# Block 2's attention: one VectorE step placed behind the maxima of the first two heads

## The chip, the cores and the metric

The kernel runs on one core of a Trainium2 chip. The time is device time in microseconds of one execution; lower is better. The kernel before takes 1686.93 us, the median of three runs (1686.88 to 1688.33).

## What is computed

Two blocks of a sequence model in float32, 256 tokens of width 1024. The second block has two layers with a context stream of another 256 tokens; only layer 0 updates the context. The part that matters is each layer's attention with eight heads: queries and keys of 96 features, the last 32 of which are turned by a rotary embedding, then softmax and a weighted sum.

```python
def apply_axial_rope(u, cos, sin):
    def rot(p):
        h = p.shape[-1] // 2
        return jnp.concatenate([-p[..., h:], p[..., :h]], axis=-1)
    rotated = jnp.concatenate([rot(u[..., :AXIS_DIM]), rot(u[..., AXIS_DIM:])], axis=-1)
    return (u.astype(jnp.float32) * cos + rotated.astype(jnp.float32) * sin).astype(u.dtype)
...
    def attend(qblk):
        logits = jnp.einsum('bqhd,bkhd->bhqk', qblk, k).astype(jnp.float32) * SM_SCALE
        p = jax.nn.softmax(logits, axis=-1).astype(v.dtype)
        return jnp.einsum('bhqk,bkhd->bqhd', p, v)
```

In layer 0 the latent queries see 512 keys and the context queries 256; in layer 1 there are latent queries alone. Next to the attention each layer has two convolution branches whose taps run on VectorE.

## The kernel before

Each engine has its own instruction stream, written out by hand, and the streams meet at semaphores ("flags"). All weights come as 460 pieces of 512 KB through a ring of eight slots, loaded by SyncE. For block 2 the streams are `l2_pe` (TensorE), `l2_act` (ScalarE) and `l2_dve` (VectorE), called once for each layer, `l` = 0 and 1. The functions named below are local to them.

**TensorE.** The up-projections write queries, keys and values; `rotations(g)` (L1749) multiplies four heads' queries (g = 0: heads 0 to 3, g = 1: heads 4 to 7) by a constant matrix into PSUM banks 4, 5 or 6, 7. Then comes a loop over heads `i` (16 in layer 0, 8 in layer 1): `scores(i + 2)`, `turned(i)`, every second time `out_pair(i - 2)`, and steps of the convolution branches (`branch_pe`). `scores(i)` (L1815) writes the scores of a head for two blocks of 128 queries into banks 0, 1 (even heads) or 2, 3 (odd heads); from head 2 on it waits for the exponentials of head i - 2 (`p_exp`), and before head 4 for the second rotation (`q_rotated`). `turned(i)` (L1825) transposes the probabilities into banks 4 and on; it waits for `p_ready` of head i. `out_pair` (L1838) multiplies by the values into bank 6, and the branch step `mean` (L1847) writes bank 7; both wait for `rotation_read`, the flag that VectorE has read the second rotation. `mean` stands behind `turned(1)` in layer 0 and behind `turned(0)` in layer 1.

**ScalarE.** `exp(i)` (L1986) takes the exponentials of a head from PSUM with the negative maximum as bias; it waits for `s_max` of head i. The loop copies the transposed probabilities to SBUF (L2032) and then does `exp(i + 2)`.

**VectorE.** `top(i)` waits for the scores (`s_ps`), takes the maxima of both query blocks in one reduction (L2206) and scales them (L2207, `s_max`). `normalised(i)` waits for `p_exp`, takes a reciprocal (L2212) and scales the probabilities (L2214 twice, `p_ready`). `rotate(g, step)` applies the rotation of four heads in three pieces of 32 partitions by 1024 elements: piece 0 (L2266) multiplies the TensorE product in PSUM by the sines into a scratch tile and waits until it is done, piece 1 (L2269) multiplies the queries by the cosines, piece 2 (L2271) adds the two. Convolution taps are L2098, L2104 and L2105; L337 splits a piece of weights. The order is that of the code:

```python
        rotate(1, 0)
        top(0)
        top(1)
        normalised(0)
        rotate(1, 1)
        for i in range(len(L.heads)):
            if i + 2 < len(L.heads):
                top(i + 2)
            if i + 1 < len(L.heads):
                normalised(i + 1)
            if i == 0:
                rotate(1, 2)
```

In front of this stand the first rotation (`rotate(0, 0)` to `rotate(0, 2)`) and the last taps. VectorE runs its instructions in this order, so an instruction that waits holds everything behind it.

Of the kernel before, what the change touches and what calls it, by code (L numbers as in the profile page):

```python
# [149 lines left out]
def program(nc, xT_in, ctxT_in, weights, params_in, shared_in, hyb_in, out):  # L150
# [144 lines left out]
    def flag(name):  # L295

        if name not in flags:
            flags[name] = sem(name)
        return flags[name]
# [1777 lines left out]
    def l2_dve(dve, link, L):  # L2077
# [31 lines left out]
        def do_taps(n):  # L2109
            for _ in range(min(n, len(taps))):  # L2110
                f, i, j = taps.pop(0)

                other = next((q for q, t in enumerate(taps) if t[:2] != (f, i)), 0)
                if taps:
                    taps.insert(0, taps.pop(other))
                if (f, i) in tap_of:
                    dve.wait_ge(flag("taps"), tap_of[f, i])
                tap_done.append(0)
                tap_of[f, i] = len(tap_done)
                f(i, j).then_inc(flag("taps"), 1)  # L2120
# [81 lines left out]
        def top(i):  # L2202
            n = 4 if L.heads[i][0] == 0 else 2
            dve.wait_ge(flag("s_ps"), L.at + i + 1)
            two = slice(2 * i, 2 * i + 2)
            link(nc.vector.tensor_reduce(c_soft[:, 0, two], psum[:, 2 * (i % 2):2 * (i % 2) + 2, 0:n * P], AX.X, ALU.max))  # L2206
            nc.vector.tensor_scalar(c_soft[:, 1, two], c_soft[:, 0, two], -SM_SCALE, None, ALU.mult).then_inc(flag("s_max"), 1)  # L2207

        def normalised(i):
            n = 4 if L.heads[i][0] == 0 else 2  # L2210
            dve.wait_ge(flag("p_exp"), 2 * (L.at + i + 1))
            link(nc.vector.reciprocal(c_soft[:, 3, 2 * i:2 * i + 2], c_soft[:, 2, 2 * i:2 * i + 2]))  # L2212
            for b in range(2):
                last = nc.vector.tensor_scalar(c_p[:, i % 2, b, 0:n * P], c_p[:, i % 2, b, 0:n * P],  # L2214
                                               c_soft[:, 3, 2 * i + b:2 * i + b + 1], None, ALU.mult)
            last.then_inc(flag("p_ready"), 1)
# [41 lines left out]
        def rotate(g, step):  # L2258

            q = c_Q[R, 4 * g:4 * g + 4, 0:SEQ]  # L2260
            turned = psum[R, 4 + 2 * g:6 + 2 * g, :].rearrange("p b c -> p (b c)").rearrange("p (h t) -> p h t", h=4)
            t = normed[R, :, :].rearrange("p a b -> p (a b)").rearrange("p (h t) -> p h t", h=4)
            four = lambda ap: ap.unsqueeze(1).broadcast_to([QK - NOPE, 4, SEQ])
            if step == 0:
                dve.wait_ge(flag("q_rot"), 2 * l + g + 1)
                nc.vector.tensor_tensor(t, turned, four(sin2), ALU.mult).then_inc(flag("rotation_read"), 1)  # L2266
                dve.wait_ge(flag("rotation_read"), 2 * l + g + 1)
            if step == 1:
                link(nc.vector.tensor_tensor(q, q, four(cos2), ALU.mult))  # L2269
            if step == 2:  # L2270
                link(nc.vector.tensor_tensor(q, q, t, ALU.add))  # L2271
                dve.sem_inc(flag("q_rotated"), 1)

        for i in range(3):
# [3 lines left out]
                    rotate(0, step)  # L2278
                branch_dve("taps")
            do_taps(6)  # L2280
        rotate(1, 0)
        top(0)
        top(1)
        normalised(0)
        rotate(1, 1)
        for i in range(len(L.heads)):
# [57 lines left out]
    with nc.Block() as block:  # L2344
# [91 lines left out]
        @block.vector  # L2436
        def _(dve):
            link = Link(dve, dve_step)
            hyb_dve(dve, link)
            layer_norm_dve(dve, link, 0, 0, "ln1_g", "ln1_b", 0, None)  # L2440
            lo_split(dve, U_MLP1 + WIDE_FIRST)
            link(nc.vector.tensor_scalar(y[:, :, 0:SEQ], x[:, :, 0:SEQ], ALPHA, None, ALU.mult))
            mlp_dve(dve, link, 0, U_MLP1, SEQ)
            layer_norm_dve(dve, link, 1, 1, "ln2_g", "ln2_b", 1, None)
            lo_split(dve, U_REC + WIDE_FIRST)
            rec_dve(dve, link, 1)
            layer_norm_dve(dve, link, 2, 2, "ln1_g", "ln1_b", 3, None)
            lo_split(dve, U_MLP2 + WIDE_FIRST)
            link(nc.vector.tensor_scalar(y[:, :, 0:SEQ], x[:, :, 0:SEQ], ALPHA, None, ALU.mult))
            mlp_dve(dve, link, 1, U_MLP2, SEQ)  # L2450
            layer_norm_dve(dve, link, 3, 3, "ln2_g", "ln2_b", None, U_L2 + LEAD)
            for L in LAYERS:
                modulated_dve(dve, L.norm, SEQ, L.split)
                l2_dve(dve, link, L)
                gated_dve(dve, link, L.norm + 1, L.T)
                modulated_dve(dve, L.norm + 2, L.T, L.split + 2)
                lo_split(dve, U_L2MLP[L.l] + WIDE_FIRST)
                dve.wait_ge(x_ready, KT * (L.split + 4))
                link(nc.vector.memset(y[:, :, 0:L.T], 0.0))
                mlp_dve(dve, link, 2 + L.l, L.base + L2_IN + 3 + KT, L.T)  # L2460
                gated_dve(dve, link, L.norm + 3, SEQ)
                if L.l == 0:
                    late_added_dve(dve)
# [198 lines left out]
```

## Time and profile before

| | |
|---|---|
| median of three runs | 1686.93 us |
| the runs | 1686.88 to 1688.33 us |
| the profiled execution's own time | 1687.68 us |
| its span (first to last instruction) | 1685.8 us |
| mean granted TensorE clock | 0.986 |
| TensorE busy | 1606.9 us (95%) |
| VectorE busy | 1027.2 us (61%) |
| ScalarE busy | 838.2 us (50%) |

The profile is of one execution. A row of the timeline gives start, duration, engine, line, operation, output and inputs, and in brackets the idle time before it with what ended it. The chain of waits is the work that ended last, followed back from the last instruction: each piece is what released the next one. PE is TensorE, DVE is VectorE, ACT is ScalarE. The granted clock is a share of TensorE's full clock of 2.4 GHz.

### The profile page before, as it was taken

The numbers are of one execution on the slowest core, as the hardware profiler recorded it, in microseconds if no ns is written. First come the engines' busy times: TensorE is split into PE (matmuls) and PEld (weight loads), VectorE is DVE, ScalarE is ACT, GpSimd is POOL, SyncE is SP. The second block draws the span as 40 slices with busy tenths as digits, with TensorE's granted clock in tenths as the row PEclk, the third lists the DMA queues.
The fourth block names the chain that finished last, engine by engine and source line by source line (L and its number), as shares of the span: only waits on it lengthen the run. The fifth ranks groups of instructions, "written<-read, shape, count | busy, mean of one in ns | idle before, by whom it ended". The sixth has DMA issues, their size and how long they took to land.

```text
span 1685.8 us, 25551 instructions
## 1 busy us (share of the span) xinstructions
PE 1606.9 (95%) x10226; PEld 1379.5 (82%) x10226; DVE 1027.2 (61%) x1616; ACT 838.2 (50%) x1484; POOL 76.6 (5%) x60
## 2 busy tenths in 40 slices
PE   7998999999999999999889999999999989889997
PEld 7887789998889999988557588888888875779996
DVE  6855765567676566769864643333333688565665
ACT  5434275554726566453684551514243555665554
POOL 1200300001031000000000100000000100100000
PEclk9999999999999999999999999999999999999999
DMA  8733665556746555543101532222222241235551
GB/s 302 264 115 138 251 235 176 187 187 225 264 174 221 180 188 187 180 158 100 63 1 63 212 101 97 91 100 87 100 100 88 67 146 38 68 122 178 185 186 50
DMA packets 69937, 247.49 MB, mean 147 GB/s; under 512 B 7504, under 2 KB 10576, under 8 KB 69712
## 3 DMA queue, kind: packets, MB, share of 16 engines
q1 hardware_dynamic: 69840, 246.18, 42.7%
q8 instruction: 63, 1.03, 0.3%
q14 instruction: 34, 0.28, 0.1%
HBM read 245.10 MB, written 1.05 MB: 146 GB/s over the span
## 4 chain that ended last, share of the span: by engine, by line
PE 75%; DVE 12%; issue 7%; ACT 4%; DMA 0%; POOL 0%; DVEq 0%; SPq 0%; ACTq 0%; POOLq 0%
PE psum L376 15%; PE psum L378 15%; PE psum L377 15%; PE psum L397 9%; PE psum L398 5%; DVE lo_ring L337 3%; PE psum L1143 2%; PE psum L1815 2%; PE psum L411 1%; DVE c_conf L2098 1%; PE psum L412 1%; PE psum L413 1%; PE psum L1825 1%; PE psum L1838 1%; PE psum L511 1%
## 5 line engine op out<-in xcount | busy, mean ns | idle before, releaser
L376 PE MATMUL psum<-x_parts,hi_ring 128*128 128x256 f32 (+1 forms) x1464 | 460.9, 315 | 12.3 <-DVE x_parts L902 9.9
L337 DVE TENSOR_TENSOR lo_ring<-raw_ring,hi_ring 128x1024 fp32r<-128x1024 f32 x348 | 432.6, 1244 | 60.2 <-PE psum L378 21.1
L377 PE MATMUL psum<-x_parts,hi_ring 128*128 128x256 f32 (+1 forms) x1464 | 456.1, 312 | 0.0
L378 PE MATMUL psum<-x_parts,lo_ring 128*128 128x256 f32 (+1 forms) x1464 | 455.9, 311 | 0.0
L349 ACT ACTIVATE hi_ring<-raw_ring 128x1024 fp32r<-128x1024 f32 x292 | 307.3, 1053 | 256.7 <-PE psum L378 137.7
L376 PEld LDWEIGHTS psum<-x_parts,hi_ring 128*128 128x128 f32 x1464 | 281.2, 192 | 34.2 <-issue 16.4
L377 PEld LDWEIGHTS psum<-x_parts,hi_ring 128*128 128x128 f32 x1464 | 281.4, 192 | 14.9 <-issue 0.2
L378 PEld LDWEIGHTS psum<-x_parts,lo_ring 128*128 128x128 f32 x1464 | 281.2, 192 | 14.8
L397 PE MATMUL psum<-hid_parts,hi_ring 128*128 128x512 f32 x672 | 235.2, 394 | 0.3 <-DVE lo_ring L337 0.3
L1420 DVE TENSOR_TENSOR hid_parts<-relu,hid_parts 128x256 fp32r<-128x256 f32 (+1 forms) x128 | 63.1, 493 | 221.1 <-ACT relu L1409 221.1
L398 PE MATMUL psum<-hid_parts,lo_ring 128*128 128x256 f32 x672 | 188.3, 280 | 0.0
L397 PEld LDWEIGHTS psum<-hid_parts,hi_ring 128*128 128x128 f32 x672 | 126.5, 188 | 29.2 <-DVE lo_ring L337 0.6
L2390 POOL TENSOR_SCALAR hi_ring<-raw_ring 128x1024 fp32r<-128x1024 f32 x56 | 76.4, 1366 | 1403.0 <-DMA raw_ring<-weights 637.7
L1406 ACT ACTIVATE relu<-psum 128x256 f32<-128x256 f32 (+1 forms) x128 | 55.7, 435 | 162.5 <-PE psum L378 149.4
L398 PEld LDWEIGHTS psum<-hid_parts,lo_ring 128*128 128x128 f32 x672 | 125.9, 187 | 0.0
L376 PE MATMUL psum<-hid_parts,hi_ring 128*128 128x512 f32 (+1 forms) x320 | 115.1, 360 | 0.0
L378 PE MATMUL psum<-hid_parts,lo_ring 128*128 128x512 f32 (+1 forms) x320 | 114.6, 358 | 0.0
L377 PE MATMUL psum<-hid_parts,hi_ring 128*128 128x512 f32 (+1 forms) x320 | 113.7, 355 | 0.0
L1449 DVE TENSOR_TENSOR y<-psum,y 128x512 f32<-128x512 f32 (+1 forms) x44 | 26.2, 595 | 110.1 <-PE psum L378 96.6
L411 PE MATMUL psum<-x_parts,hi_ring 128*128 128x256 f32 (+1 forms) x184 | 59.7, 324 | 14.8 <-DVE x_parts L1195 9.0
L1443 DVE TENSOR_TENSOR y<-psum,y 128x256 f32<-128x256 f32 x84 | 35.7, 425 | 59.1 <-PE psum L398 53.8
L2098 DVE SCALAR_TENSOR_TENSOR c_conf<-c_u,par,c_conf 128x512 f32<-128x512 f32 (+1 forms) x120 | 68.3, 617 | 0.9
(430 smaller groups left out, 2338.2 us busy)
## 6 DMA issues: line engine op xcount, KB each, us to landing
raw_ring<-weights SPq DMA_DIRECT2D x460, 512.0 KB, 3.4
h_const<-hyb_consts SPq DMA_DIRECT2D x1, 1088.0 KB, 11.4
x<-xT SPq DMA_DIRECT2D x1, 1024.0 KB, 6.9
x<-ctxT SPq DMA_DIRECT2D x1, 1024.0 KB, 16.6
outT<-x SPq DMA_DIRECT2D x4, 256.0 KB, 2.5
shared<-shared_consts SPq DMA_DIRECT2D x1, 398.0 KB, 13.3
par<-params SPq DMA_DIRECT2D x1, 301.5 KB, 7.0
```

The source lines that it names most:

```text
L337: nc.vector.tensor_tensor(lo_ring[:, s, :], raw_ring[:, UNIT_AT[u] % RAW_SLOTS, :], hi_ring[:, s, :].bitcast(F32), ALU.subtract).then_inc( ...
L349: nc.scalar.activation(hi_ring[:, SPLIT[v] % SPLIT_SLOTS, :], raw_ring[:, slot, :], ACT.Copy).then_inc(act_hi_ready, 1)
L376: nc.tensor.matmul(bank(u % BANKS, T), w_hi, hi[:, hi_place[k], 0:T], start=(k == 0), stop=False)
L377: nc.tensor.matmul(bank(u % BANKS, T), w_hi, lo[:, k, 0:T], start=False, stop=False)
L378: last = nc.tensor.matmul(bank(u % BANKS, T), w_lo, hi[:, hi_place[k], 0:T], start=False, stop=(k == KT - 1))
L397: nc.tensor.matmul(side_by_side(u), w_hi, parts[:, :, k, 0:SEQ], start=(k == 0), stop=False)
L398: last = nc.tensor.matmul(bank(u % BANKS, SEQ), w_lo, parts[:, 0, k, 0:SEQ], start=False, stop=(k == KT - 1))
L411: nc.tensor.matmul(bank(v % BANKS, T), w_hi, hi[:, hi_place[k], 0:T], start=(k == order[0]), stop=False)
L1406: nc.scalar.activation(relu[:, j % 2, 0:T], bank(u % BANKS, T), ACT.Relu).then_inc(drained[u % BANKS], 1)
L1420: nc.vector.tensor_tensor(hid_lo[:, j, 0:T], relu2[:, j % 2, 0:T], hid_hi[:, j, 0:T].bitcast(F32), ALU.subtract).then_inc(flag("hidden_rea ...
L2098: return nc.vector.scalar_tensor_tensor(acc, src, w, acc, ALU.mult, ALU.add)
L2390: nc.gpsimd.tensor_scalar(hi_ring[:, n % SPLIT_SLOTS, :], raw_ring[:, slot, :], 1.0, 0.0, ALU.mult, ALU.add).then_inc(hi_ready, 1)
```

## The change

In `l2_dve`, for both layers, piece 0 of the second rotation moves behind the maxima of heads 0 and 1.

```diff
             do_taps(6)
-        rotate(1, 0)
         top(0)
         top(1)
+        rotate(1, 0)
         normalised(0)
         rotate(1, 1)
```

## Rows read from the trace of the kernel before

**Rows 1.** The page: busy time by engine (part 1), the chain by engine (part 4).
```profile
PE 1606.9 (95%) x10226; PEld 1379.5 (82%) x10226; DVE 1027.2 (61%) x1616; ACT 838.2 (50%) x1484; POOL 76.6 (5%) x60
...
PE 75%; DVE 12%; issue 7%; ACT 4%; DMA 0%; POOL 0%; DVEq 0%; SPq 0%; ACTq 0%; POOLq 0%
```

**Rows 2.** Chain of waits, layer 1: start us, us, engine, tile, line.
```profile
1410.15 1.23 DVE normed L2266
...
1411.41 1.24 DVE c_soft L2206
...
1412.87 1.46 ACT c_p L1986 x4
...
1414.37 3.78 PE psum L1815 x4
...
1425.76 1.06 PE psum L1825 x8
...
1434.99 1.02 ACT c_pT_low L2032
```

**Rows 3.** Chain of waits, layer 0.
```profile
831.57 1.24 DVE c_soft L2206
...
833.10 0.88 DVE c_p L2214 x2
...
834.01 1.23 DVE c_Q L2269
...
835.26 1.24 DVE c_soft L2206
...
836.52 0.17 DVE c_soft L2207
...
836.79 0.89 DVE c_p L2214 x2
...
837.82 1.06 PE psum L1825 x8
...
856.88 1.02 ACT c_pT_low L2032
```

**Rows 4.** Timeline of all engines, layer 0.
```profile
828.39 1.22 DVE L2266 TENSOR_TENSOR normed<-psum,shared 32x1024 f32<-32x1024 f32 x1
...
829.93 1.23 DVE L2206 TENSOR_REDUCE c_soft<-psum 128x2 f32<-128x1024 f32 x1 [0.32 <-PE psum L1815]
...
832.89 1.98 PE L1815 MATMUL psum<-c_K,c_Q 96*128 96x512 f32 x4 [1.36 <-ACT c_p L1986]
```

**Rows 5.** Timeline of all engines, layer 1.
```profile
1408.05 3.70 PE L1815 MATMUL psum<-c_K,c_Q 96*128 96x512 f32 x8 [1.48 <-DVEq L2272]
...
1414.35 0.17 DVE L2212 RECIPROCAL c_soft<-c_soft 128x2 f32<-128x2 f32 x1 [0.18 <-ACT c_p L1986]
1414.37 3.78 PE L1815 MATMUL psum<-c_K,c_Q 96*128 96x512 f32 x4 [2.62 <-ACT c_p L1986]
```

**Rows 6.** Busy time by stretch: columns as in the first line.
```profile
core 0: us, PE busy (x) PEld busy (x) DVE busy (x) ACT busy (x) POOL busy (x), PEclk, DMA share, GB/s
831.55:832.89 1.34, 0.00 (x0) 0.00 (x0) 1.29 (x2) 1.29 (x4) 0.00 (x0) 1.00 0.00 0
832.89:840.50 7.61, 7.26 (x29) 4.02 (x30) 7.23 (x14) 4.86 (x10) 0.00 (x0) 1.00 0.00 0
862.18:864.83 2.65, 0.00 (x0) 0.00 (x0) 0.00 (x0) 2.64 (x6) 0.00 (x0) 1.00 0.00 0
864.83:868.24 3.41, 3.37 (x12) 2.91 (x13) 2.20 (x7) 3.02 (x7) 0.00 (x0) 0.50 0.00 0
...
1411.75:1414.37 2.62, 0.00 (x0) 0.00 (x1) 2.37 (x5) 1.50 (x5) 0.00 (x0) 1.00 0.00 0
1414.37:1421.20 6.83, 6.83 (x16) 4.39 (x17) 5.08 (x10) 2.59 (x6) 0.00 (x0) 0.50 0.00 0
```

## The prediction

> **What bounds the kernel now.** I read the page's busy times and its chain first, to see which engine ends the kernel; then the chain of waits and the timeline over the start of block 2's attention in each of its two layers; last the granted clock there. TensorE is busy 95% of the span and holds 75% of the chain, VectorE 61% and 12% [rows 1]. Averaged so, VectorE looks harmless. But at the start of attention there are no scores yet, TensorE has nothing else to do, and the chain passes through VectorE. The change sits there, and the two layers must be read apart, because in them the moved step meets opposite conditions.
>
> Layer 1 (around 1410 us): VectorE is late. It runs the step to be moved, rotate(1, 0), from 1410.15, then the maxima of head 0 at 1411.41; these release ScalarE's exponentials (1412.87), and these release the scores of head 2 (1414.37) [rows 2]. All of this is on the chain, and TensorE idles 2.62 us before the scores of head 2 [rows 5].
>
> Layer 0 (around 830 us): VectorE is early. It starts rotate(1, 0) at 828.39 and then still waits 0.32 us for the scores of head 0 before the maxima at 829.93 [rows 4]. So the step is hidden under TensorE's first scores. From 831.57 the chain leaves TensorE and runs through VectorE alone: maxima of head 1, normalising of head 0, rotation, maxima of head 2, normalising of head 1, up to the transposes of head 1 at 837.82 [rows 3].
>
> **The change part by part.** Nothing is added or removed: one VectorE instruction (1.22 us, 1.26 from its start to the next one's, 1410.15 to 1411.41 [rows 2, 4]) changes its place in the queue, together with its two waits. The wait for TensorE's rotation matmuls is met in both places: the step starts at 828.39 and 1410.15 with no idle time shown before it, and its new place is later. The wait for its own completion travels with it and lies inside the 1.26. The bank that it reads is released later, but the matmuls that need this bank also stand behind transposes that need normalised probabilities, and VectorE gives those only after the step. No DMA and no other queue is moved; the weight stream moves nothing in the listed stretches (0 GB/s) [rows 6].
>
> *Layer 0: a loss of 1.26.* In front, taking the step away gives nothing: the maxima of head 0 wait for the scores anyway. Behind the maxima of head 1 (which end with the small scaling after 831.57 + 1.26) the step stands in the VectorE chain and pushes each later item by 1.26: normalising of head 0 from 833.10 to 834.36, transposes of head 1 from 837.82 to 839.08 [rows 3]. Behind the step now queue the normalising of head 0, whose transposes TensorE waits for, and the maxima of head 2, which ScalarE waits for. From 837.82 the chain holds only TensorE up to 856.88, where ScalarE takes over from it [rows 3]; there is no slack that could take the 1.26 back. Bounds: nothing below zero, since nothing starts earlier, and 1.26 above. I take 1.26, because the chain has no idle time to absorb it.
>
> *Layer 1: a gain.* The maxima of head 0 move from 1411.41 to 1410.15, for the scores of head 0 are there by then: TensorE began its eight score instructions at 1408.05 and needs 3.70 for both heads [rows 5], half of it by 1409.90. The exponentials of head 0 then come at 1411.61 instead of 1412.87 and the scores of head 2 at 1413.11 instead of 1414.37: 1.26 earlier. The idle time of TensorE shrinks from 2.62 to 1.36. The maxima of head 1 wait for their scores until 1411.77 (1408.05 + 3.70), and the step follows; it ends at about 1414.45, and normalising of head 0, which stood at 1414.35 waiting for exponentials [rows 5], moves by 0.1 only. So the step now fills time in which VectorE waited.
>
> The second part of the gain depends on the clock. In the kernel before the granted clock is 1.00 during the 2.62 us of idle and 0.50 (1.2 GHz instead of 2.4) from 1414.37 to 1421.20 [rows 6]: the scores of head 2 take 3.78 there against 1.98 for the same four instructions in layer 0 [rows 4, 5]. In layer 0 TensorE idles 1.36 at this very place and the clock stays at 1.00 [rows 4, 6]. With the change layer 1 has layer 0's idle time, so I take it that the clock stays up. Then VectorE becomes the chain, item by item from layer 0's starts [rows 3]: from 1411.77 maxima of head 1 with scaling 1.45, the step 1.26, normalising 1.10, rotation 1.25, maxima of head 2 1.26, normalising with its preparation 1.16, rotation 1.25, maxima of head 3 1.26, normalising 1.16, and 0.14 to TensorE: the transposes of head 2 start at 1423.06 instead of 1425.76 [rows 2], a gain of 2.70. From there the chain of before has only TensorE until ScalarE at 1434.99 [rows 2], which moves with it. If the clock falls all the same, the gain is the 1.26 of the earlier start. Bounds: 1.26 and 2.70; I take 2.70, by the row nearest to it, the idle time of 1.36 in layer 0 at full clock.
>
> *What the skill would say.* The Trainium skill ("TensorE: Matmul & The Clock Gate", A second HAM failure mode: psum-queue depth-cycling) tells of a kernel in which frequent short idle times between groups of matmuls that cycle through PSUM banks made the clock swing; the scores here cycle through two pairs of banks. By that page the sum would be 0.0 rather than -1.4; layer 0's stretch speaks against it.
>
> *Sum.* 1.26 - 2.70 = -1.44. The profiled execution took 1687.68 (span 1685.8), 0.75 above the median of 1686.93; its own time would become 1686.24. The change of -1.44 set against the median gives **1685.5 us**.
>
> **The rivals.**
> *A: the clock falls in layer 1 anyway*, after idle times of 1.48 and 1.36 so close together [rows 5]. Then +1.26 - 1.26 = 0: 1686.9. For it: the first of the two gaps has no counterpart in layer 0. Against it: layer 0.
> *B: nothing moves, because VectorE isn't the engine that counts.* The Trainium skill ("Perfetto Trace Analysis", Identifying the Most-Contended Engine) wants the engine with the highest occupancy improved first, which by the page of the profile is not VectorE. Time: 1686.9. Against it: the chain names VectorE at both places [rows 2, 3]; only an exact cancelling gives this time, which is A.
> *C: a further half-clock stretch goes.* In layer 0 TensorE idles 2.65 from 862.18 and then has 0.50 until 868.24 [rows 6]. Work that comes 1.26 later may meet the clock otherwise. Such a stretch, 3.37 busy at half clock, is worth 1.7: 1683.8; with a second one 1682.1.
> *D, slower: the clock falls in layer 0.* The step opens new idle time of TensorE before the transposes of heads 0 and 1, about 0.7 and 1.1, behind the 1.36. If this brings 0.50 as in layer 1, a stretch of 6.83 [rows 6] costs up to 3.4; with layer 1's sure 1.26 this is +1.26 + 3.4 - 1.26: 1690.3; half of that stretch 1688.6. It decides where the clock after 832.89 is below 1.00. Against it: each gap is at most 1.36, which the row shows harmless alone.
>
> **How the numbers follow.** Forecast 0.52; A 0.22; B 0.03; C 0.14; D 0.09. The three times shown differ by up to 1.45 (1686.88 to 1688.33), so a median can be off by half that, 0.7. A measurement can tell about 0.2%, 3.4 us, from no change. The range goes from C's 1683.8 less 0.7, 1683.1, to D's milder 1688.6. Faster by over 3.4 needs C with a second stretch or with the spread: 0.09. Slower by over 3.4 needs D in full: 0.04. The rest, 0.87, is no measurable change.
>
> **What would show it.** Right: in layer 1 the maxima of head 0 start at about 1410.15 plus layer 0's shift, TensorE's idle time before the scores of head 2 is near 1.36, the clock from there on is 1.00, and the transposes of head 2 come 2.7 earlier against the first scores. In layer 0 the transposes of head 1 come at about 839.1 with some 1.1 idle before them, chained to VectorE. Wrong: a clock of 0.50 behind the scores of head 2 (A), or behind 832.89 (D); transposes of head 1 in layer 0 still at 837.8; or an equal time in which both layers moved by other amounts than these.

## The result, and the profile after

The kernel after takes 1689.02 us, the median of 20 runs (1685.88 to 1695.10); the kernel before beside it takes 1686.18, also 20 runs (1682.89 to 1689.17). The ratio is 1.0023, with a 95% interval of 1.0014 to 1.0032: slower by 2.4 to 5.4 us, 2.8 by the medians. The forecast was 1685.5, and its range ended at 1688.6: wrong in sign and outside the range.

The profiled execution took 1686.86 (span 1684.9, mean granted clock 0.986), which is 0.8 less than that of before and 2.2 less than its own median. So one trace against one trace shows the wrong sign here. What hides it lies in front of the change: the last piece of the first rotation in layer 0, up to which both kernels run the same instructions, starts at 824.34 after and at 826.13 before, and from there to the end of the span the traced execution after takes 860.6 against 859.6. The reading below therefore goes by stretches in several traces. The page of after, engines and chain (answers to [rows 1]):

```profile
PE 1605.9 (95%) x10226; PEld 1377.0 (82%) x10226; DVE 1027.1 (61%) x1616; ACT 838.1 (50%) x1484; POOL 75.2 (4%) x60
...
PE 79%; DVE 9%; issue 7%; ACT 4%; DMA 1%; POOL 0%; SPq 0%; DVEq 0%; ACTq 0%; POOLq 0%
```

VectorE's share of the chain fell from 12% to 9% and TensorE's busy time by 1.0. Both look like progress. The chain of waits after, both layers (answers to [rows 2, 3]):

```profile
829.78 1.24 DVE c_soft L2206
...
831.24 1.23 DVE normed L2266
...
832.70 0.38 DVE c_p L2214
...
1406.29 3.71 PE psum L1815 x8
...
1410.03 1.24 DVE c_soft L2206
...
1411.49 1.23 DVE normed L2266
...
1413.86 1.23 DVE c_Q L2269
```

In both layers the moved step (L2266) is now a link of the chain: in layer 0 it was not one, in layer 1 it was one before the maxima and is one behind them. The timeline after, of all engines (answers to [rows 4, 5]):

```profile
828.07 1.22 DVE L2206 TENSOR_REDUCE c_soft<-psum 128x2 f32<-128x1024 f32 x1 [1.61 <-PE psum L1815]
...
831.04 0.17 DVE L2207 TENSOR_SCALAR c_soft<-c_soft 128x2 f32<-128x2 f32 x1
...
831.24 1.22 DVE L2266 TENSOR_TENSOR normed<-psum,shared 32x1024 f32<-32x1024 f32 x1
...
837.42 1.06 PE L1825 MATMUL psum<-shared,c_p 128*128 128x128 f32 x8 [0.97 <-DVE c_p L2214]
...
1406.29 3.70 PE L1815 MATMUL psum<-c_K,c_Q 96*128 96x512 f32 x8 [1.48 <-DVEq L2272]
...
1411.36 1.98 PE L1815 MATMUL psum<-c_K,c_Q 96*128 96x512 f32 x4 [1.36 <-ACT c_p L1986]
...
1412.75 0.17 DVE L2212 RECIPROCAL c_soft<-c_soft 128x2 f32<-128x2 f32 x1
...
1416.37 0.17 DVE L2207 TENSOR_SCALAR c_soft<-c_soft 128x2 f32<-128x2 f32 x1
...
1416.45 0.16 DVE L2212 RECIPROCAL c_soft<-c_soft 128x2 f32<-128x2 f32 x1
...
1421.48 1.06 PE L1825 MATMUL psum<-shared,c_p 128*128 128x128 f32 x8 [0.61 <-DVE c_p L2214]
...
1439.05 1.39 PE L1825 MATMUL psum<-shared,c_p 128*128 128x128 f32 x8 [2.85 <-DVE c_p L2214]
...
1440.37 3.25 PE L1838 MATMUL psum<-c_pT_low,c_v 128*64 128x256 f32 x16
```

The same place in the trace of before, behind the same idle time:

```profile
1443.34 1.06 PE L1825 MATMUL psum<-shared,c_p 128*128 128x128 f32 x8 [2.85 <-DVE c_p L2214]
1444.33 1.95 PE L1838 MATMUL psum<-c_pT_low,c_v 128*64 128x256 f32 x16
```

Where the step was taken away in layer 0, VectorE now only waits (1.61 before the maxima of head 0). In layer 1 the scores of head 2 take 1.98 again behind 1.36 of idle time, as forecast. But behind the transposes of head 6 the products with the values take 3.25; in the trace of before the same 16 take 1.95. Busy time by stretch after, columns as in [rows 6]:

```profile
826.15:832.89 6.74, 5.46 (x13) 2.01 (x11) 4.67 (x8) 2.90 (x9) 0.00 (x0) 1.00 0.00 0
831.03:837.42 6.39, 4.79 (x17) 2.21 (x17) 6.11 (x12) 3.57 (x8) 0.00 (x0) 1.00 0.00 0
...
1411.36:1421.48 10.12, 8.71 (x33) 4.50 (x33) 9.64 (x18) 6.04 (x13) 0.00 (x0) 1.00 0.00 1
...
1439.65:1443.06 3.41, 3.41 (x19) 1.92 (x19) 1.76 (x5) 2.20 (x5) 0.00 (x0) 0.50 0.02 5
...
1487.44:1494.26 6.82, 5.83 (x27) 5.86 (x28) 4.18 (x9) 6.38 (x13) 0.00 (x0) 0.50 0.00 1
```

The half-clock stretch behind the scores of head 2 is gone, and two stand further on that the trace of before does not have: at the transposes of head 6 and at the beginning of layer 1's MLP.

To compare whole stretches, the starts of the same VectorE instruction (at 1501, of a wait) are taken in every trace. The times below are differences of such starts, named by their place in the trace of before. Layer 0's first stretch goes from the last piece of the first rotation (826.13) to the last piece of the second (837.70); layer 1's goes from the tap behind the first rotation (1408.08) to the maxima of head 3 (1423.20).

| stretch (us of before) | before | after |
|---|---|---|
| 826 to 837, start of layer 0's attention | 11.58 | 12.96 |
| 857 to 900, its end | 42.87 | 44.50 |
| 1408 to 1423, start of layer 1's attention | 15.12 | 12.59 |
| 1423 to 1441 | 17.70 | 17.71 |
| 1441 to 1450, transposes of head 6 | 9.93 | 11.56 |
| 1450 to 1476 | 25.20 | 25.20 |
| 1476 to 1490, second normalisation | 14.18 | 14.48 |
| 1490 to 1501, beginning of the MLP | 11.05 | 12.49 |
| 1408 to 1501 together | 93.18 | 94.03 |

So layer 1 gains 2.53 at its start and gives back 1.63, 0.30 and 1.44 before 1501, 3.37 in all.

### The profile page after: what moved, and what is told of

The parts are those of the page before. It is cut to its first block, busy times and chain, and to the rows that moved or that the text cites. A ratio compares the mean times of both kernels' runs of the same rounds, so it can differ in the third digit from the quotient of the medians.

```text
span 1684.9 us, 25551 instructions
## 1 busy us (share of the span) xinstructions
PE 1605.9 (95%) x10226; PEld 1377.0 (82%) x10226; DVE 1027.1 (61%) x1616; ACT 838.1 (50%) x1484; POOL 75.2 (4%) x60
## 4 chain that ended last, share of the span: by engine, by line
PE 79%; DVE 9%; issue 7%; ACT 4%; DMA 1%; POOL 0%; SPq 0%; DVEq 0%; ACTq 0%; POOLq 0%
PE psum L376 16%; PE psum L378 15%; PE psum L377 15%; PE psum L397 9%; PE psum L398 5%; PE psum L1143 2%; PE psum L424 2%; PE psum L411 2%; DVE lo_ring L337 2%; PE psum L413 1%; PE psum L412 1%; PE psum L1815 1%; PE psum L1838 1%; PE psum L511 1%; PE psum L1825 1%
```

## The experiments

Three theories were to be told apart. **Order:** layer 1 is faster by its new order, and what is lost is layer 0's 1.39 and work elsewhere. **Clock:** layer 1's shorter start is nothing but the missing half-clock stretch, and half-clock stretches that come later instead take it back. **Scatter:** the later stretches differ from execution to execution whatever the order. The expectations on record name their theories by letters; what a letter stands for is told by what it expects. All ratios are against the kernel before, run beside it on the same chip, with 95% intervals.

### One layer at a time, and the kernel after again

```diff
-        rotate(1, 0)
+        if l != 0:
+            rotate(1, 0)
         top(0)
         top(1)
+        if l == 0:
+            rotate(1, 0)
```

This is layer 0 alone; the kernel for layer 1 alone has 1 in place of 0. The kernel after ran beside them.

> The step moves in layer 0 alone. Theory P (the arithmetic of the prediction, and the rest is elsewhere): +1.3 us. Theory Q (in some executions the clock falls at the start of layer 0's attention, because the moved step opens new idle time of TensorE there): +3 us or more in the median, with single executions 5 us and more above the others. Theory R (the clock falls in layer 1 instead): +1.3 us.

> The step moves in layer 1 alone. Theories P and Q: faster by 1.3 to 2.7 us, and without executions far above the others. Theory R: slower by 1.5 us or more, with single executions 5 us above.

> The changed kernel once more, for another trace and other executions. All theories: about +2.8 us against before, single executions at 1692 us or more; if the trace is of one of these it shows where the half-clock stretch lies (Q: behind 830 us, R: behind 1410 us, P: in neither).

| | median us (range, runs) | ratio |
|---|---|---|
| before | 1686.25 (35 runs) | |
| layer 0 alone | 1688.62 (1683.42 to 1692.66, 12) | 1.0014 [1.0001, 1.0027] |
| layer 1 alone | 1686.49 (1682.53 to 1690.58, 12) | 1.0001 [0.9989, 1.0012] |
| after, again | 1691.22 (1683.57 to 1694.05, 12) | 1.0018 [1.0004, 1.0032] |

The part in layer 0 is slower, by an interval that just leaves out no change; the part in layer 1, forecast to gain 2.70, shows no gain. For layer 1 alone none of the three theories had forecast an equal time. The start of layer 0's attention takes 12.96 with layer 0 alone and 11.57 with layer 1 alone: the 1.39 belongs to layer 0's move. In layer 1 alone the start of layer 1's attention took 14.28 and not 12.59, because this time the clock was halved earlier, at the first scores. Its timeline:

```profile
1406.14 5.40 PE L1815 MATMUL psum<-c_K,c_Q 96*128 96x512 f32 x8 [1.48 <-DVEq L2272]
```

The eight took 5.40 instead of 3.70. The transposes of head 6 cost 1.63 more there too, and 1408 to 1501 took 94.06, against 93.19 with layer 0 alone, where layer 1 has the old order.

### Filling the idle time before the scores of head 2

```diff
         scores(1)
+        for f in range(3):
+            nc.tensor.matmul(psum[:, 4, :], c_Q[0:QK, 0, 0:P], c_K[0:QK, 0, 0:TB], start=True, stop=True)
```

Here the kernel after has three more matmuls in each layer, whose result nobody reads, so that TensorE does not idle before the scores of head 2.

> The changed kernel with three matmuls whose output nobody reads behind the scores of head 1, in both layers: they fill the idle time of 1.3 us before the scores of head 2 and add no wait. Theories Q and R: the executions at 1692 us and more go, and the median comes to 1.4 us below before or lower. Theory P: the spread stays, the median stays at +2.8 us or is a little above.

1687.84 (1683.26 to 1692.83, 12 runs), ratio 1.0011 [0.9998, 1.0025]: between before and after, and not told from either. Its trace again has half clock at the first scores (start 14.28) and at the transposes of head 6 (11.56), and 1408 to 1501 takes 95.59. Filling this one place does not keep the clock up.

### Single traces: how much differs without any change

The kernel before was traced twice more, layer 1 alone, layer 0 alone and the kernel after once more each. No edit; one time each.

> The kernel before, for a second trace. Theory S (in layer 1 the old order lets the clock fall at the scores of head 2, and then not at the second long idle time, in front of the transposes of head 6; with the step moved it falls there instead): half clock behind the scores of head 2 and 1.00 behind the transposes of head 6, as in the first trace; the first scores of layer 1 to the copy of the last head pair take 42.5 us. Theory U (where the clock falls is a matter of the single execution and has nothing to do with the order): in this trace it may fall at either place, at both or at none.

> The kernel before, for a third trace. Theory V says where half clock can be, at the idle times of 2.6 to 3.1 us, but not in which execution. If the old order ties its places together (theory S): half clock behind the scores of head 2 in layer 1 and none at the second normalisation behind the attention, as in both traces so far.

> The step moves in layer 1 alone, for a second trace. Theory S: 1.00 behind the scores of head 2, half clock behind the transposes of head 6, about 1.6 us given back there. Theory U: either.

> The step moves in layer 0 alone, second trace. Theories X and V: 1.39 us lost between the step's place and the probabilities of head 1. Behind it, from 857 to 892 us: if the new order makes more half clock there, 28.5 us or more between the maxima of head 5 and those of the last head (with 26.9 where the clock stays up); if it is a matter of the execution alone, about as often 26.9 as 28.3 or more.

> The changed kernel, third trace. Layer 0 as in the run before it. Layer 1, theory X: no half clock behind the scores of head 2, half clock at the transposes of head 6, and from the last instruction of the first rotation to the second normalisation's end 93.9 us or more (before: 93.2 to 93.4 in four traces).

The times were 1684.95 (before again), 1688.84 (before, third), 1685.82 (layer 1 alone), 1691.47 (layer 0 alone) and 1690.21 (after, third). The table puts all traces in which the idle times at head 6 and behind are not filled beside each other; head 2 filled is the kernel of the last experiment. The stretch from 826 to 837 has no column: it is 11.57 or 11.58 with the old order in layer 0 and 12.96 or 12.97 with the new one, in every trace.

| trace | 857 to 900 | 1372 to 1395 | 1408 to 1423 | 1441 to 1450 | 1490 to 1501 | 1408 to 1501 | 1372 to 1501 |
|---|---|---|---|---|---|---|---|
| before | 42.87 | 22.87 | 15.12 | 9.93 | 11.05 | 93.18 | 128.53 |
| before again | 43.11 | 21.50 | 13.81 | 11.48 | 11.05 | 93.40 | 127.39 |
| before, third | 42.88 | 22.86 | 15.11 | 9.94 | 11.06 | 93.20 | 128.54 |
| layer 0 alone | 41.63 | 22.87 | 15.13 | 9.92 | 11.05 | 93.19 | 128.54 |
| layer 0 alone, again | 47.22 | 21.52 | 15.14 | 9.93 | 11.05 | 93.23 | 127.24 |
| after | 44.50 | 21.55 | 12.59 | 11.56 | 12.49 | 94.03 | 128.07 |
| after, again | 45.63 | 21.57 | 12.59 | 11.56 | 12.47 | 93.93 | 127.98 |
| after, third | 41.64 | 21.36 | 14.28 | 11.56 | 12.47 | 95.65 | 129.49 |
| after, filled | 41.64 | 21.34 | 14.28 | 11.56 | 12.46 | 95.59 | 129.41 |
| layer 1 alone | 44.46 | 21.34 | 14.28 | 11.56 | 11.04 | 94.06 | 127.88 |
| layer 1 alone, again | 43.03 | 21.53 | 12.59 | 11.56 | 11.23 | 93.00 | 127.01 |
| head 2 filled | 44.50 | 22.87 | 12.44 | 11.56 | 12.56 | 94.10 | 129.45 |

The stretches of layer 1 are coupled. In the four traces with the long stretch behind the scores of head 2 (start 15.1) the transposes of head 6 keep full clock (9.9), and in all eight others they don't (11.5 to 11.6). From 1408 to 1501 the five traces with the old order and nothing filled take 93.2 to 93.4, the six with the new one 93.0 to 95.7, 94.4 on average. A part of that difference is not the order's: the half clock at the first scores (14.28) comes before the step's place makes any difference, and in layer 1 alone nothing in front of it is changed; it goes with a shorter stretch further up, 21.34 to 21.36 from 1372 to 1395. Counted from 1372 the means are 128.05 and 128.31, and the ranges overlap (127.24 to 128.54 and 127.01 to 129.49). So by the means the gain of 2.5 at the start is taken back in full, and by how much more lies between 0.3 and 1.1; from so few traces it may also be nothing.

Much of the scatter arises in front of the change: the last piece of the first rotation in layer 0, with only the same instructions in front of it, starts between 823.61 and 829.49 in these twelve traces. From there to the end of the span the three traces of before take 857.4 to 859.8 and the three of after 860.6 to 861.7, 2.1 more by the means.

Scatter is real, then, but it is not the whole: head 6 loses its full clock in every trace with the new order. Before again shows the exchange without any change: its half-clock stretch at head 2 is half as long, and the second one comes at head 6. Its busy time by stretch:

```profile
1411.57:1414.98 3.41, 3.41 (x6) 1.24 (x6) 2.07 (x3) 1.07 (x4) 0.00 (x0) 0.50 0.00 0
1438.88:1442.29 3.41, 3.27 (x16) 2.41 (x18) 1.37 (x4) 2.42 (x6) 0.00 (x0) 0.50 0.00 0
```

After, third, shows a clock that was halved at the first scores. Busy time by stretch:

```profile
1408.85:1412.25 3.40, 3.40 (x5) 1.35 (x4) 2.24 (x4) 0.00 (x0) 0.00 (x0) 0.50 0.02 5
...
1442.98:1446.40 3.42, 3.42 (x18) 2.05 (x17) 1.59 (x5) 2.28 (x5) 0.00 (x0) 0.50 0.00 0
1490.77:1497.60 6.83, 5.79 (x27) 5.82 (x28) 4.18 (x9) 6.36 (x13) 0.00 (x0) 0.50 0.00 1
```

The end of layer 0's attention (857 to 900) takes 42.9 to 44.5 in the six traces above with the old order there, and 41.6 to 47.2 with the new one. In layer 0 alone, again, two full stretches at half clock stand in it:

```profile
868.66:875.50 6.84, 6.62 (x16) 4.46 (x17) 3.03 (x9) 5.14 (x14) 0.00 (x0) 0.50 0.01 2
892.55:899.38 6.83, 6.05 (x24) 3.32 (x21) 2.53 (x6) 3.04 (x6) 0.00 (x0) 0.50 0.00 0
```

The spread is wider with the new order; whether its mean is higher can't be told from six traces a side.

### Filling the idle times behind

First, in the kernel with layer 1 alone, the long idle time before the transposes of head 6: a step of the convolution branch moves there, led by five matmuls whose result nobody reads.

```diff
-                 {0: ["mean"], 3: ["sums"], 4: ["sc"], 7: ["again"]}]
+                 {0: ["mean"], 3: ["sums"], 5: ["sc"], 7: ["again"]}]
...
+        def idle_fill(b, n):
+            for _ in range(n):
+                nc.tensor.matmul(psum[:, b, 0:2 * P], c_Q[0:QK, 4, 0:P], c_K[0:QK, 0, 0:2 * P], start=True, stop=True)
...
                 pe.wait_ge(flag("branch_rstd"), 2 * l + 1)
+                idle_fill(7, 5 if l else 0)
```

> The step moves in layer 1 alone, and there the sums of the short convolution's squares move from head 4 to behind the transposes of head 5, led by five matmuls that nobody reads, so that TensorE has work in the long idle time in front of the transposes of head 6. Theory S: the clock stays up there, the 1.6 us come back: 1.5 to 2.5 us faster than before, and the trace shows 1.00 from 1410 to 1450. Theory U: 1.3 us faster than before or less; equal to the variant without it.

1684.45 (1681.55 to 1690.11, 12 runs), before 1686.36, ratio 0.9994 [0.9983, 1.0005]: not told from before. In its trace (lines moved by four) the idle time before the transposes of head 6 is 0.69 and they run at full clock:

```profile
1436.43 1.06 PE L1829 MATMUL psum<-shared,c_p 128*128 128x128 f32 x8 [0.69 <-DVE c_p L2219]
1437.42 1.95 PE L1842 MATMUL psum<-c_pT_low,c_v 128*64 128x256 f32 x16
```

The 1.63 is gone: 1423 to 1450 takes 27.63, as before (17.70 + 9.93), against 29.27 after. But 1476 to 1490 now takes 15.47 instead of 14.18, with half clock from 1474.63: the stretch went one idle time further on.

Then the same in layer 0 (its step moves from head 5 to head 6, with four matmuls), three more before the transposes of head 14 there, and three before layer 1's first scores:

```diff
+        if l:
+            pe.wait_ge(flag("job_read"), L.jobs * (l + 1))
+            for _ in range(3):
+                nc.tensor.matmul(psum[:, 3, 0:2 * P], c_Q[0:QK, 4, 0:P], c_K[0:QK, 0, 0:2 * P], start=True, stop=True)
         pe.wait_ge(flag("q_rotated"), 2 * l + 1)
...
+            if (l, i) == (0, 14):
+                pe.wait_ge(flag("branch_rstd"), 2 * l + 2)
+                idle_fill(7, 3)
             turned(i)
```

> As the run before, and three more long idle times of TensorE are filled in the same way: before the scores of head 9 and before the transposes of head 14 in layer 0, before the first scores in layer 1. Both theories: no half clock between 830 and 890 and between 1404 and 1450 in the trace; by the half-clock stretches seen there (1.3 to 1.6 us each) 3 to 5 us faster than before. If the filling itself is in the way: no faster than the run before.

1681.38 (1679.21 to 1682.31, 5 runs), ratio 0.9967 [0.9954, 0.9980]: faster than both kernels.

### The order alone, with the clock kept up

To compare the orders without the clock, the fillings above go into three kernels that differ in the step's place, with twelve more matmuls around layer 1's second normalisation. Only the one with the old order in both layers also has five before the scores of head 2:

```diff
         scores(1)
+        if l:
+            for _ in range(5):
+                nc.tensor.matmul(psum[:, 4, 0:2 * P], c_Q[0:QK, 0, 0:P], c_K[0:QK, 0, 0:2 * P], start=True, stop=True)
...
+                if L.l:
+                    for _ in range(6):
+                        nc.tensor.matmul(psum[:, 7, 0:SEQ], ones[:, :], sc("cos2", SEQ), start=True, stop=True)
                 norm_pe(pe, L.norm + 2, L.T)
                 if L.l == 0:
                     mods(pe, "post_sum")
+                else:
+                    for _ in range(6):
+                        nc.tensor.matmul(psum[:, 7, 0:SEQ], ones[:, :], sc("cos2", SEQ), start=True, stop=True)
```

> The old order in both layers, with TensorE's long idle times filled by matmuls that nobody reads: as in the run before, and also behind the scores of head 1 in layer 1 and twice in the normalisations behind layer 1's attention. Theory V (the arithmetic of the queues holds where the clock stays up: the step's new place costs 1.4 us in layer 0 and gains 1.3 us in layer 1, the start alone; all the rest of the measured difference is half clock at one place or another): no half clock between 830 and 890 and between 1404 and 1495, 1.3 us slower than the next run, 5 us faster than before. Theory W (the rest is not the clock): about 1 to 2 us faster than before, or slower.

> The step moves in layer 1 alone, with the same idle times filled (but not the one behind the scores of head 1). Theory V: the fastest of the three, 6 to 7 us faster than before; against the old order with the fillings 1.3 us faster, all of it between the first scores and the maxima of head 3 in layer 1. Theory W: the order does not matter here.

> The step moves in both layers, with the same idle times filled. Theory V: 1.4 us slower than the run before it, all of it between the step's place and the probabilities of head 1 in layer 0; 5 us faster than before. Theory W: slower than the old order with the fillings by more than 2 us.

| filled, with | median us (range, runs) | ratio | 826 to 837 | 1408 to 1423 | 1408 to 1501 |
|---|---|---|---|---|---|
| old order | 1681.85 (1677.39 to 1682.99, 6) | 0.9967 [0.9955, 0.9979] | 11.58 | 12.44 | 90.44 |
| new in layer 1 | 1680.37 (1679.59 to 1682.60, 5) | 0.9965 [0.9952, 0.9978] | 11.58 | 12.59 | 90.61 |
| new in both | 1683.26 (1681.87 to 1686.09, 10) | 0.9985 [0.9976, 0.9994] | 12.97 | 12.59 | 90.60 |

In all three traces the granted clock is 1.00 from 829 to 890 and from 1404 to 1495. The result falls against the order theory. With full clock the old order needs 12.44 for the start of layer 1's attention and the new one 12.59: the new place gains nothing and costs 0.15. The timeline of the old order filled (lines moved by 8 on TensorE, by 15 on VectorE) shows why:

```profile
1403.96 3.70 PE L1823 MATMUL psum<-c_K,c_Q 96*128 96x512 f32 x8 [0.18 <-DVEq L2287]
...
1406.07 1.22 DVE L2281 TENSOR_TENSOR normed<-psum,shared 32x1024 f32<-32x1024 f32 x1
...
1410.27 0.17 DVE L2227 RECIPROCAL c_soft<-c_soft 128x2 f32<-128x2 f32 x1 [0.19 <-ACT c_p L2001]
1410.29 1.98 PE L1823 MATMUL psum<-c_K,c_Q 96*128 96x512 f32 x4 [0.47 <-ACT c_p L2001]
...
1412.64 1.23 DVE L2221 TENSOR_REDUCE c_soft<-psum 128x2 f32<-128x1024 f32 x1
```

The step is in front again (1406.07). The reciprocal that begins the normalising of head 0 starts 6.31 after the first scores; in after it is 6.46 (1406.29 to 1412.75), in before 6.30 (1408.05 to 1414.35 [rows 5]). VectorE does the same work up to there in either order. The scores of head 2 are needed only later: even in the old order they are done at 1412.27 (1410.29 + 1.98) with the clock up, before VectorE comes to their maxima at 1412.64. In before, at half clock, they were done at 1418.15 (1414.37 + 3.78).

By rows, the new order in both layers with full clock costs 1.39 + 0.15 = 1.5; the medians differ by 1.4. For layer 1 alone the medians can't decide: 1680.37 is 1.5 below the old order's 1681.85, near the 1.3 of theory V, but these are five and six runs that spread over 3.0 and 5.6, and the two ratios, 0.9965 and 0.9967, can't be told apart. The stretch of 12.59 against 12.44 decides.

### The first part of this alone: the old order with head 2 filled

The last question was whether the give-back in layer 1 needs the new order at all, or only the missing stretch. The kernel before gets the five matmuls before the scores of head 2 in layer 1 (the first part of the diff above) and nothing else.

> The kernel before with its order kept; only in layer 1 five matmuls that nobody reads stand behind the scores of head 1. Theory X (the step costs VectorE the same in both places of layer 1, and the shorter start of the changed kernel is the missing half-clock stretch alone): 12.4 us from the last instruction of the first rotation to the maxima of head 3 (before: 15.1, changed: 12.6), half clock at the transposes of head 6 as in the changed kernel, so that 1.6 us or more of the 2.7 are given back; the median within 1.5 us of before. Theory P (the step's place gives 1.3 us of it): 13.7 us or more there.

1689.65 (1684.58 to 1693.65, 12 runs), before 1686.95, ratio 1.0014 [1.0003, 1.0026]: slower, although nothing was reordered and its start of layer 1's attention is the shortest, 12.44. Its timeline and busy time by stretch:

```profile
1419.36 1.98 PE L1815 MATMUL psum<-c_K,c_Q 96*128 96x512 f32 x4 [0.46 <-ACT c_p L1989]
...
1445.64 1.08 PE L1825 MATMUL psum<-shared,c_p 128*128 128x128 f32 x8 [2.85 <-DVE c_p L2217]
1446.65 3.57 PE L1838 MATMUL psum<-c_pT_low,c_v 128*64 128x256 f32 x16
```

```profile
1413.04:1424.00 10.96, 10.50 (x37) 6.36 (x38) 10.25 (x18) 4.53 (x12) 0.00 (x0) 1.00 0.01 1
1446.57:1449.98 3.41, 3.41 (x18) 1.73 (x16) 1.93 (x5) 1.87 (x4) 0.00 (x0) 0.50 0.00 0
1494.35:1501.18 6.83, 5.99 (x28) 6.02 (x29) 4.18 (x9) 6.30 (x13) 0.00 (x0) 0.50 0.00 1
```

Full clock at head 2, then half clock at the transposes of head 6 (3.57 instead of 1.95 for the 16 products) and at the MLP's beginning, as in after. So the give-back comes with the missing stretch and without the new order. Theory X was right in the stretches and missed the median, which lies 2.7 above before and not within 1.5. From 1408 to 1501 the one trace is 0.9 longer than the mean of the old order (94.10 against 93.24); where the rest of the 2.7 lies is not shown.

## Why the prediction was wrong

**Layer 0, a loss of 1.26: right, and somewhat small.** 1.39 in all seven traces with the step moved there, 0.00 in all with it in place. In after the chain needs 2.92 from the maxima of head 1 to the normalising of head 0 (829.78 to 832.70), before 1.53 (831.57 to 833.10 [rows 3]). The missing 0.13: the step starts only when the small scaling in front of it is done (831.04 + 0.17, then 831.24), whereas a reciprocal starts 0.08 behind it (1416.37, 1416.45). The Trainium skill ("VectorE: DVE Perf Modes", Two Vector instructions with no wait between them) has a rule for this, given there as a model: an instruction whose input or output begins in another quadrant of partitions than the last access is held until all earlier ones are done. The step works on the last 32 of 96 partitions, the scaling on all 128; the rows agree.

**Layer 1, the local forecast: right in half of the traces.** In after the maxima of head 0 start 2.11 after the first scores instead of 3.36, the idle time is 1.36, the clock stays at 1.00, and the transposes of head 2 come 15.19 after the first scores instead of 17.71: 2.52 of the 2.70. In three of six traces with this order the clock was halved at the first scores instead, behind the 1.48 (start 14.28). Rival A named this idle time as the doubtful one, but placed the half clock behind the next.

**The step that failed is the 2.70 itself**, in three of its sentences. "If the clock falls all the same, the gain is the 1.26 of the earlier start": earlier scores of head 2 are worth nothing, by 12.44 against 12.59. "So the step now fills time in which VectorE waited": the forecast had itself found that the normalising of head 0 "moves by 0.1 only", and that was the sign that the step stayed on VectorE's chain, only at another place in it. "From there the chain of before has only TensorE until ScalarE at 1434.99 [rows 2], which moves with it": the chain moves, but not its clock. The 2.5 are a half-clock stretch that was avoided, and behind later idle times (in after 2.85 before the transposes of head 6 and 3.10 at the beginning of the MLP) half clock comes where it did not come before. A sum that takes the rest of the kernel as it stands in one trace can't see that.

**The sum.** 1.39 in layer 0, sure; layer 1 a gain of 2.5 that is given back with 0.3 to 1.1 on top, by the means of six and five traces whose ranges overlap (layer 1 alone measured 1.0001). That is 1.7 to 2.5 of the measured 2.8; the three traces a side, counted from 826 to the end, give 2.1. The rest, and what the end of layer 0's attention adds (41.6 to 47.2), stays open, and so does why an avoided stretch brings a later one: the runs show that it does, not by what rule.

**The rivals.** B drew on the Trainium skill ("Perfetto Trace Analysis", Identifying the Most-Contended Engine), which wants the most occupied engine improved first. The time did not stay where it was, so B did not happen; but the one thing that made the kernel faster was done to TensorE, 0.9967 by filling its idle times, so in direction the rule and the runs agree. C's stretch in layer 0 did go in some traces (41.6 instead of 42.9) and doubled in others (47.2). D had the sign, not the mechanism: the clock is 1.00 from 826.15 to 837.42 in after. The sentence on the Trainium skill's depth-cycling section ("TensorE: Matmul & The Clock Gate") pointed the right way, a price for short idle times paid in the clock, but not to the place: in after the clock stays at 1.00 while the scores cycle through their banks (1411.36 to 1421.48) and is halved at the transposes of head 6, behind 2.85.

**The spread.** The range took 1.45 from three runs; twenty runs spread over 6.3 before and 9.2 after. With that, a shift of 2.8 could be outside a range made from three. Much of this spread arises in front of the change, where the same instructions took from 823.61 to 829.49.

## What to carry to other kernels

An instruction that is moved on a chained engine helps only if something else then starts earlier and is needed earlier: compare the next join of both chains (here the normalising of head 0) before counting any earlier start. A stretch at half clock was not, in this kernel, a cost that an edit removes for good: filling one idle time of TensorE made it slower (1.0014), filling the long ones of this part, with a branch step moved into them, made it faster (0.9967). Where the clock differs from execution to execution, compare stretches between the same instructions over several traces, leave out what lies in front of the change, and never take the sign from one trace a side.

## What the runs showed of the hardware that was not expected

The place of the half-clock stretches differs between executions of one kernel: the start of layer 1's attention took 15.12, 13.81 and 15.11 in three traces of the kernel before, with nearly the same total (93.18 to 93.40). The half-clock stretches shown above lasted 3.4 or 6.8. The same idle time of 1.48 before layer 1's first scores was followed by half clock in three of the table's six traces with the new order there and by full clock in the other three and in its six with the old order, though no work in front of it differs in layer 1 alone. So that idle time alone does not decide what the clock does behind it. The half clock went with a shorter stretch further up (21.34 to 21.36 from 1372 to 1395, against 21.50 and more where the clock stayed up); why, is open.
